# Conv taps waiting by quarter, masked keys on GpSimd, and one copy for two PSUM banks in a two-layer decoder step

## What is computed

```python
def mixer(h, past_k, past_v, s0, buf, past_len, p):
    z = h @ p['w_in']
    ...                       # split into gq, gk, gv, gg, glr, sq, sk, sv, cu
    o_gla, s_new = gla_chunked(q, k, v, log_a, s0)          # S = exp(b_last) * S + khat^T v
    ...
    o_sb = stick_breaking(q_sb, k_all, v_all, ...)          # past keys and values from 16 pages a row
    a, gate = jnp.split(cu, 2, axis=-1)
    u = a * jax.nn.sigmoid(gate)
    y, buf_new = causal_dwconv(u, buf, p['conv_w'], p['conv_b'])   # 31 taps over 256 channels
    y = jax.nn.silu(layer_norm(y, p['conv_norm_g'], p['conv_norm_b']))
    return concatenate([o_gla, o_sb, y]) @ p['w_out'], ...
```

## Time and profile before

| | |
|---|---|
| median of 3 runs | 1406.13 us (1405.67 to 1406.16) |
| the profiled execution | 1406.77 us, its span 1405.1 us |
| granted TensorE clock, mean | 0.998 |
| TensorE busy | 1381.3 us, 98% |
| VectorE, ScalarE, GpSimd busy | 899.9, 735.0, 182.6 us |

### The profile page before, as it was taken

How to read it: one execution, slowest core, us unless ns; L and a number is a source line. 1 busy time by engine, 2 the same in 40 slices (tenths; PEclk the granted TensorE clock), 3 DMA queues, 4 the chain that set the end, 5 groups by cost and what they waited for, 6 DMA issues and landing times.

```text
span 1405.1 us, 27974 instructions
## 1 busy us (share of the span) xinstructions
PE 1381.3 (98%) x11063; PEld 1302.6 (93%) x11063; DVE 899.9 (64%) x1508; ACT 735.0 (52%) x1210; POOL 182.6 (13%) x333
## 2 busy tenths in 40 slices
PE   7999999999999999999999999999999999999998
PEld 6999999977878999999999999999788799999998
DVE  5666544669995866663367665346899858756542
ACT  4544343489866554443355444346887665444441
POOL 1020000323262110000000000012333510000000
PEclk9999999999999999999999999999999999999999
DMA  9475455567798595545555554564868895555541
GB/s 245 144 209 150 143 147 157 159 197 229 216 317 262 145 255 150 149 142 150 153 132 151 150 150 139 152 181 139 250 207 252 286 255 155 150 150 148 149 139 50
DMA packets 391558, 249.47 MB, mean 178 GB/s; under 512 B 16513, under 2 KB 379638, under 8 KB 391428
## 3 DMA queue, kind: packets, MB, share of 16 engines
q1 hardware_dynamic: 375602, 204.94, 51.2%
q0 software_dynamic: 15520, 42.62, 9.6%
q10 hardware_dynamic: 306, 0.13, 0.1%
HBM read 242.10 MB, written 5.53 MB: 176 GB/s over the span
## 4 chain that ended last, share of the span: by engine, by line
PE 92%; ACT 2%; DVE 2%; issue 1%; DMA 1%; SPq 0%; POOL 0%; POOLq 0%; DVEq 0%; ACTq 0%
PE bank L605 24%; PE bank L607 24%; PE bank L606 24%; PE bank L763 2%; PE bank L988 2%; PE bank L641 2%; PE bank L645 2%; PE bank L642 2%; PE bank L892 2%; PE bank L1065 1%; ACT kT L1411 1%; DMA raw<-in_ffn_w_gate 1%; PE bank L845 1%; PE bank L969 1%; PE bank L1183 1%
## 5 line engine op out<-in xcount | busy, mean ns | idle before, releaser
L1617 DVE TENSOR_TENSOR w_l<-raw,w_h 128x1024 fp32r<-128x1024 f32 (+1 forms) x332 | 395.6, 1197 | 290.7 <-ACT w_h L1239 290.3
L605 PE MATMUL bank<-hh,w_h 128*128 128x320 f32 x1632 | 513.0, 314 | 0.0
L607 PE MATMUL bank<-hh,w_l 128*128 128x320 f32 x1632 | 504.2, 309 | 0.0
L606 PE MATMUL bank<-hl,w_h 128*128 128x320 f32 x1632 | 504.1, 309 | 0.0
L1239 ACT ACTIVATE w_h<-raw 128x1024 fp32r<-128x1024 f32 (+1 forms) x332 | 332.5, 1030 | 141.2 <-DMA raw<-in_ffn_w_down 100.1
L605 PEld LDWEIGHTS bank<-hh,w_h 128*128 128x128 f32 x1632 | 306.3, 188 | 12.5 <-issue 7.8
L606 PEld LDWEIGHTS bank<-hl,w_h 128*128 128x128 f32 x1632 | 306.5, 188 | 0.6
L607 PEld LDWEIGHTS bank<-hh,w_l 128*128 128x128 f32 x1632 | 306.4, 188 | 0.0
L605 PE MATMUL bank<-guh,w_h 128*128 128x320 f32 x704 | 217.7, 309 | 0.0
L607 PE MATMUL bank<-guh,w_l 128*128 128x320 f32 x704 | 217.3, 309 | 0.0
L606 PE MATMUL bank<-gul,w_h 128*128 128x320 f32 x704 | 217.3, 309 | 0.0
(11 more groups left out here) (295 smaller groups left out, 1581.4 us busy)
## 6 DMA issues: line engine op xcount, KB each, us to landing
raw<-in_ffn_w_gate SPq DMA_DIRECT2D x88, 512.0 KB, 3.9
raw<-in_ffn_w_up SPq DMA_DIRECT2D x88, 512.0 KB, 3.9
raw<-in_ffn_w_down SPq DMA_DIRECT2D x64, 448.0 KB, 3.7
raw<-in_w_in SPq DMA_DIRECT2D x44, 512.0 KB, 3.9
raw<-in_ffn_w_down SPq DMA_DIRECT2D x32, 512.0 KB, 4.0
kpg<-in_cache_sb_k SPq DMA_DIRECT2D x112, 128.0 KB, 3.3
kpg<-in_cache_sb_k POOLq DMA_DIRECT2D x112, 128.0 KB, 2.6
raw<-in_w_out SPq DMA_DIRECT2D x16, 512.0 KB, 6.9
```

What stands on the lines that cost most here:

```text
L605: pe.matmul(out, w_h[:, slot, k, :], rhs_h[:, k0 + k, :], start=first, stop=False)
L606: pe.matmul(out, w_h[:, slot, k, :], rhs_l[:, k0 + k, :], start=False, stop=False)
L607: last = pe.matmul(out, w_l[:, slot, k, :], rhs_h[:, k0 + k, :], start=False, stop=end)
L1617: V(dve.tensor_tensor(w_l[:, slot, 0:n, :], raw[:, slot, 0:n, :], w_h[:, slot, 0:n, :].bitcast(F32), ALU.subtract), sm["w_lo"])
```

## The change

Three edits in one kernel.

- conv: `V.settle()` remains only at tap 0. From tap 1 on, each of the four instructions waits for the instruction of its own quarter in the tap before (`tapped`).
- knm is computed by GpSimd, behind `values(3)` in its list and ahead of `values(4)`, behind a wait for knat_ready; the VectorE instruction is gone.
- Banks 2 and 3 are allocated as one tensor, turned, and `copy_keys` reads both in one instruction of 1024 columns, which counts kt_copied by two. `Steps` takes the amount as an argument.

```diff
--- before.py
+++ after.py
@@ -192,10 +192,10 @@
     def __init__(self, eng, own):
         self.eng, self.own, self.count, self.last = eng, own, {}, None
 
-    def __call__(self, ins, sem=None):
+    def __call__(self, ins, sem=None, by=1):
         sem = self.own if sem is None else sem
-        ins.then_inc(sem, 1)
-        self.count[sem.name] = self.count.get(sem.name, 0) + 1
+        ins.then_inc(sem, by)
+        self.count[sem.name] = self.count.get(sem.name, 0) + by
         self.last = (sem, self.count[sem.name])
         return ins
 
@@ -343,7 +343,10 @@
         lo, hi = AT[name]
         return const[0:rows, lo:hi if cols is None else lo + cols]
 
-    bank = [stack.enter_context(nc.psum_tensor(f"bank{i}", [P, 512], F32)) for i in range(8)]
+    bank = [stack.enter_context(nc.psum_tensor(f"bank{i}", [P, 512], F32)) for i in range(2)]
+    turned = stack.enter_context(nc.psum_tensor("turned", [P, 2, 512], F32))
+    bank += [turned[:, 0], turned[:, 1]]
+    bank += [stack.enter_context(nc.psum_tensor(f"bank{i}", [P, 512], F32)) for i in range(4, 8)]
     sm = {name: stack.enter_context(nc.semaphore(name)) for name in SEMAPHORES.split()}
     w_loaded = [sm[f"w_loaded{s}"] for s in range(SLOTS)]
     per = per_layer()
@@ -569,6 +572,10 @@
                         store_rows("v", svn)
                 for it in range(ITS):
                     values(it)
+                    if it == 3:
+                        pool.wait_ge(*at("knat_ready", 2))
+                        pool.tensor_tensor(knm[:, :, :], kn[0:TS, 2:3, :].to_broadcast([TS, DB, 256]),
+                                           cst_("batch_of", TS).unsqueeze(2).to_broadcast([TS, DB, 256]), ALU.mult).then_inc(sm["knm_ready"], 1)
                 pool.wait_ge(*at("s2_ready", 2))
                 pool.dma_start(outs["prompt_gla_state"][l, 0].rearrange("(p h) k v -> (h k) p v", p=2), s2[:, :, :]).then_inc(so, 16)
                 pool.wait_ge(*at("st_done", 16))
@@ -1404,11 +1411,12 @@
 
                     if h in KEYS_EARLY[l]:
                         return
-                    for b in batches:
-                        act.wait_ge(*at("kt_turned", 4 * h + b - b % 2 + 2))
-                        if h >= 2:
-                            act.wait_ge(*at("kt_used", h - 1))
-                        A(nsa(half_keys(kT[l][:, h % 2], b), turned_half(2 + b % 2), ACT.Copy), sm["kt_copied"])
+                    b0 = batches[0]
+                    act.wait_ge(*at("kt_turned", 4 * h + b0 + 2))
+                    if h >= 2:
+                        act.wait_ge(*at("kt_used", h - 1))
+                    dst = kT[l][:, h % 2, b0:b0 + 2].rearrange("p b a c -> p (b a c)").rearrange("p (n t s) -> p t n s", t=2, s=64)
+                    A(nsa(dst, turned[:, :, :].rearrange("p t (n s) -> p t n s", s=64), ACT.Copy), sm["kt_copied"], 2)
 
                 def place_scores(it):
 
@@ -1790,9 +1798,12 @@
                 ffn(2 * l, 3 * l, U)
                 settle_in(M1, U + U_IN)
 
+                tapped = {}
+
                 def conv(k):
 
-                    V.settle()
+                    if k == 0:
+                        V.settle()
                     for c in range(2):
                         v = ext[:, c, HALO + TP:].rearrange("p (b t) -> p b t", b=DB)[:, :, k:k + DT]
                         for n, (out, x) in enumerate(((yT[:, c, 0:TP], ext[:, c, k:k + TP]),
@@ -1800,9 +1811,10 @@
                             if k == 0:
                                 V(dve.tensor_scalar(out, x, par("conv_w", c), par("conv_b", c), ALU.mult, ALU.add))
                             else:
+                                dve.wait_ge(*tapped[c, n])
                                 V(dve.scalar_tensor_tensor(out, x, par("conv_w", 2 * k + c), out, ALU.mult, ALU.add),
                                   sm["conv_y"] if k == TAPS - 1 and c == n == 1 else None)
-
+                            tapped[c, n] = V.last
 
                 def blocks(t, w, half=None):
 
@@ -2006,8 +2018,6 @@
                     for h in pair:
                         V(dve.tensor_tensor(fT[:, h, :], osq[:, h, :], gate[:, h, :], ALU.mult), sm["o_done"])
 
-                V(dve.tensor_tensor(knm[:, :, :], kn[0:TS, 2:3, :].to_broadcast([TS, DB, 256]),
-                                    cst_("batch_of", TS).unsqueeze(2).to_broadcast([TS, DB, 256]), ALU.mult), sm["knm_ready"])
                 if taps < TAPS:
                     conv(taps)
                 gla_read((0, 1))
```

## The result

The change made the kernel slower: 1409.6 us median of 10 runs (1408.32 to 1410.44), against 1405.9 us of the kernel before measured with it. The ratio is 1.0021, 95% interval 1.0011 to 1.0031, which is 3.0 us; the medians lie 3.7 apart. The forecast was 1411.0 with the range 1403.4 to 1412.8. What happened is case A, exclusion, at a price that was set too high.

The account below looks back on a forecast made before the run. TensorE's own work and waits were taken as the bound (busy 1381.3 of 1405.1 us). From the median, 1406.1, 6.7 us more waiting and 1.8 less, net 4.9, gave 1411.0, range 1403.4 to 1412.8.

Parts of the forecast that it names:

- case A: At TensorE's means: GpSimd's knm excludes VectorE's ps_t, TensorE waits 6.7 us more and 1.8 less, 1411.0 us; chance 0.52.
- price: TensorE's added wait at the means for ps_t held up by knm: 3.1 us plus 3.6 us, 6.7 in all.
- The length d: Duration of knm on GpSimd: 4.6 us taken, midway between two passes (3.7) and three (5.5).
- The gains: Taps and key copies together: 0.9 us a layer less waiting of TensorE, 1.8 us in all.
- The att term: TensorE's waits for VectorE's att writes: quicker conv taps take back 0.4 of 0.6 us a layer.
- The copy term: ScalarE's key copies, one for two banks: 0.06 us saved for each of 8 pairs, 0.5 us a layer.
- case B: GpSimd's knm and VectorE's ps_t pass each other or stretch within 1.06 us: only 1.8 us gained, 1404.3; chance 0.38.
- The threshold: The whole kernel is slower by over 0.2% (2.8 us) from a knm duration of 3.65 us on; chance of slower 0.46.
- The ends of case B: Range of the time if the engines pass each other: 1402.9 to 1406.5 us, with 0.05 below 1403.3.
- C: GpSimd's knm lasts beyond 6.7 us and values reach TensorE late, without exclusion: 1406.9 us at 8 us; chance 0.04.
- D: The copy over two banks is slow or the taps' many waits cost, without exclusion: 1407.7 us; chance 0.04.

Follow-up runs that it names:

- e5: The change with knm back on VectorE and two GpSimd memsets of the same columns in its place; one profiled run, ps_t 0.69 us, no ratio.
- e6: The change with knm one step earlier on GpSimd, behind values(2); one profiled run, TensorE's wait 1.19 us, no ratio.
- e2: Only knm moved to GpSimd behind values(3), taps and copies as in the kernel before; 1408.71 us, ratio 1.0013 to the kernel before.
- e1: The change without the move of knm (taps and one copy for two banks only); 1405.05 us against 1407.09, ratio 0.9983 to the kernel before.
- e8: Only the one copy for two banks, taps as before and knm on VectorE; one profiled run, first stretch 107.86 and 107.87 us, no ratio.
- e11: The change as made, measured once more without an edit; 1410.14 us, ratio 1.0019 to the kernel before.
- e10: The change with knm later in GpSimd's list, behind values(5); 1405.62 us, ratio 0.9990 to the kernel before.
- e4: The change with knm at its place on GpSimd but in four instructions of 512 columns; 1406.4 us, ratio 0.9998 to the kernel before.

## Why the prediction came out as it did

- **The mechanism and its place** were right: ps_t stands until knm ends, and TensorE stands at the means. e5, e6, e2 and e1 show each part.
- **The length d** was mis-sized: 4.6 us from midway between two and three passes at the memset's rate, measured 3.59. The end of two passes, 3.7, was the right row. With 3.6 the prediction's own sum gives 2.1 and 2.6 us of stop, 4.7 in all, for the 6.7 that it added; the stretches show 2.0 and 2.4, 4.4 in all.
- **The gains** were set at 1.8 us and are 1.0: 108.01 + 108.02 against 107.51 + 107.54. The att term (0.4 a layer) was right. The copy term (0.5 a layer, 0.06 for each of 8 pairs) was too high: the copy is as short as forecast, but with it alone (e8) the stretch is only 0.15 a layer shorter, and the waits for kT shrink by as much. Counting a saving for each pair in ScalarE's run ahead of a wait was the wrong step; at which pairs the saving is lost isn't shown.
- **The two errors partly cancel.** The price was 2.3 us too high and the gain 0.8 too high, so 4.9 was forecast and 3.4 is left, of which the two measurements show 3.0 and 2.7 (0.0021 and 0.0019 of the time). That 1411.0 lies near 1409.6 is in part luck. And a range from 1403.4 to 1412.8 would have held case B as well; what bears the forecast out is the place and the length of the stop in the traces.
- **What was missing** is the clock. It goes with most of the scatter: the 33 executions of the kernel before beside e1 average 1406.4 at a mean granted clock of 0.998 (16 of them) and 1408.3 at 0.996 (6). Between the two kernels it hardly differs (0.9977 over the 12 executions of e11, 0.9978 over the 17 of the kernel before beside them), so it isn't what makes the change slower. A fall behind the stop costs its 1.7 us, a fall ahead is swallowed.
- **The threshold** "slower by over 0.2%" stood at d = 3.65; by the sum's own terms (4.9 us falls by 2 for each us that d is under 4.6) it is 3.55. d was 3.59, so the result lies on that bound, 0.21% and 0.19%, though both intervals are clear of no change. The near even chances for slower and the same said as much.
- **The ends of case B**, 1402.9 and 1406.5, don't follow from the ends that the prediction gives for the two edits. Those are 1.4 us a layer gained or 0.8 lost, so 1403.3 and 1407.7, and the 0.05 for B below 1403.3 had no ground in them.
- **The rest of the sum** held: two taps from 2.58 to 2.44, no late values (C), no price for crossing banks (D), and VectorE's 2.3 us worth nothing to TensorE (e10 has the second stretch of the kernels with knm on VectorE, 26.39).

## What to carry to other kernels

An engine with little to do isn't a free place: before moving an instruction to GpSimd, list which VectorE instructions with two SBUF tensors fall into its span and how much slack their readers have; here 1.06 us of slack met 3.59 us of exclusion. Let it run beside VectorE instructions with at most one SBUF tensor (the four ps_z in e6). Cutting it into parts near the slack brought back about half of the loss here, not all of it (e4). Where VectorE isn't what TensorE waits for, the move gains nothing in any place (e10), and leaving knm on VectorE was best (e1). And where totals scatter by more than the effect, compare stretches between two starts on the bounding engine, with the clock's falls beside them.

## What the runs showed of the hardware

- A GpSimd instruction that reads SBUF and a VectorE instruction with two SBUF tensors exclude each other for a whole instruction: 0.69 became 3.69 us (layer 0) and 4.07 (layer 1), with the end 0.56 us behind GpSimd's. With knm in four parts GpSimd's stand behind VectorE's too, 1.48 us each for 1.03 (e4). One tensor from PSUM and one from SBUF pass beside it (1.13 us for four, as alone); two GpSimd memsets, 3.7 us together, left ps_t at 0.69 (e5).
- ScalarE's reading of two PSUM banks in one instruction shows no price for the crossing: 1.021 us for 1024 columns against 0.594 for 512, where the line through 320 and 512 columns in one bank gives 1.04.
- GpSimd multiplied two tensors of 64x2048 in 3.59 us, with the next DMA issued 3.56 us behind its start; VectorE takes 2.28.
- TensorE's granted clock fell to 1.2 GHz for 3.4 us at a time in the stretch between the prompt scores and the state products, with or without a stop ahead of it, and not in the same places in every execution of one kernel: layer 1 has such a fall in the first profile of the change and none in e11.
